# A depthwise convolution's low diagonal tiles and sampled products, moved from GpSimd and ScalarE to VectorE

## The reference

```python
def conv_module(x, prev, w1, b1, dw, dwb, lng, lnb, w2, b2):
    h = jnp.dot(x, w1) + b1
    a, gt = jnp.split(h, 2, axis=-1)
    u = a * jax.nn.sigmoid(gt)
    ext = jnp.concatenate([prev.astype(u.dtype), u], axis=1)
    c = lax.conv_general_dilated(ext, dw[:, None, :], window_strides=(1,), padding='VALID',
                                 dimension_numbers=('NWC', 'WIO', 'NWC'), feature_group_count=D_MODEL)
    c = layer_norm(c + dwb, lng, lnb)
    y = jnp.dot(jax.nn.silu(c), w2) + b2
    return y, ext[:, -CONV_CTX:]
```

## Time and profile before

| | |
|---|---|
| median of 3 runs | 1351.56 us (1350.29 to 1352.23) |
| span of the profiled execution, first to last instruction | 1350.1 us |
| TensorE, share of the span | 93% |
| VectorE | 78% |
| ScalarE | 59% |
| GpSimd | 4% |
| the depthwise stage on VectorE | about 334 to 428 us |
| the experts, all eight | about 500 to 1340 us |

### The profile page before, as it was taken

One profiled execution on the slowest core, in us unless ns is written; L12 is line 12 of the kernel. 1 busy time (PEld: TensorE's weight loads), 2 busy tenths in 40 slices (PEclk: granted clock), 3 DMA queues, 4 the chain that ended last, 5 costly groups with the idle time before them and its releaser, 6 DMA issues.

```text
span 1350.1 us, 22286 instructions
## 1 busy us (share of the span) xinstructions
PE 1262.2 (93%) x8696; PEld 1174.4 (87%) x8696; DVE 1046.8 (78%) x1016; ACT 802.5 (59%) x901; POOL 56.5 (4%) x34
## 2 busy tenths in 40 slices
PE   6999999989875989999999999999999999999993
PEld 4899999979874869999998998998998998998992
DVE  6734343469998668889889889888888888888886
ACT  3533333354653456766776766776776776776771
POOL 0000000001642000000000000000000000000000
PEclk9999999999887989999999999999999999999997
DMA  9854444253030407998998998998998998998931
GB/s 276 266 172 157 159 158 150 60 158 105 13 121 32 156 32 237 370 358 284 370 361 277 367 363 278 366 363 275 367 363 279 366 350 292 365 366 282 366 140 37
DMA packets 249538, 332.66 MB, mean 246 GB/s; under 512 B 6404, under 2 KB 222820, under 8 KB 249450
## 3 DMA queue, kind: packets, MB, share of 16 engines
q1 hardware_dynamic: 249283, 331.28, 73.2%
q10 hardware_dynamic: 199, 0.62, 0.2%
HBM read 330.44 MB, written 2.84 MB: 247 GB/s over the span
## 4 chain that ended last, share of the span: by engine, by line
PE 80%; DVE 14%; ACT 3%; issue 2%; DMA 1%; DVEq 0%; ACTq 0%
PE bank L1068 35%; PE bank L1088 18%; PE bank L889 15%; PE bank L918 6%; DVE cacc L1321 5%; PE bank L1032 2%; PE bank L1077 1%; PE bank L838 1%; DVE w_lo L1165 1%; PE bank L1053 1%; ACT w_hi L543 1%; DVE acc L1469 1%; DMA spool<-in_state_pool_dram 1%; PE bank L874 1%; DVE uc_lo L1349 1%
## 5 line engine op out<-in xcount | busy, mean ns | idle before, releaser
L1165 DVE TENSOR_TENSOR w_lo<-raw,w_hi 128x2048 fp32r<-128x2048 f32 x309 | 707.9, 2292 | 200.7 <-ACT w_hi L543 200.1
L543 ACT CAST w_hi<-raw 128x2048 fp32r<-128x2048 f32 x309 | 590.9, 1913 | 260.2 <-PE bank L889 107.6
L1068 PE MATMUL bank<-w_hi,xg_hi 128*128 128x256 f32 x1408 | 401.6, 285 | 5.3 <-DVE acc L1469 3.6
L1068 PE MATMUL bank<-w_hi,xg_lo 128*128 128x256 f32 x1408 | 394.0, 280 | 0.0
L1068 PE MATMUL bank<-w_lo,xg_hi 128*128 128x256 f32 x1408 | 393.9, 280 | 0.0
L1068 PEld LDWEIGHTS bank<-w_hi,xg_hi 128*128 128x128 f32 x1408 | 265.4, 189 | 13.2 <-issue 8.9
L1068 PEld LDWEIGHTS bank<-w_lo,xg_hi 128*128 128x128 f32 x1408 | 266.0, 189 | 3.2
L1068 PEld LDWEIGHTS bank<-w_hi,xg_lo 128*128 128x128 f32 x1408 | 265.2, 188 | 0.0
L889 PE MATMUL bank<-x_hi,w_hi 128*128 128x304 f32 (+1 forms) x544 | 166.2, 305 | 8.5 <-DVE x_lo L1252 5.3
L889 PE MATMUL bank<-x_hi,w_lo 128*128 128x304 f32 (+1 forms) x544 | 164.3, 302 | 0.0
L889 PE MATMUL bank<-x_lo,w_hi 128*128 128x304 f32 (+1 forms) x544 | 163.6, 301 | 0.0
(11 more groups left out here) (191 smaller groups left out, 1337.8 us busy)
## 6 DMA issues: line engine op xcount, KB each, us to landing
raw<-in_moe_w_gate_dram SPq DMA_DIRECT2D x88, 1024.0 KB, 5.6
raw<-in_moe_w_up_dram SPq DMA_DIRECT2D x88, 1024.0 KB, 5.9
raw<-in_moe_w_down_dram SPq DMA_DIRECT2D x88, 1024.0 KB, 5.2
raw<-in_conv_w_dram SPq DMA_DIRECT2D x12, 1024.0 KB, 5.4
raw<-in_ffn_w_gate_dram SPq DMA_DIRECT2D x11, 1024.0 KB, 8.0
raw<-in_ffn_w_up_dram SPq DMA_DIRECT2D x11, 1024.0 KB, 8.1
raw<-in_ffn_w_down_dram SPq DMA_DIRECT2D x11, 1024.0 KB, 4.9
poolw<-in_pool_w_dram SPq DMA_DIRECT2D x1, 1024.0 KB, 11.1
```

The lines of the kernel that those rows point to most:

```text
L543: act.copy(w_hi[t % SPLIT][:], raw[t % RAW][:]).then_inc(hi_ready, 1)
L1068: last = pe.matmul(bank[:, 0:TW], x[:, c, :], w[:, c, :], start=(c == 0 and k == 0), stop=(c == KC - 1 and k == 2))
L1165: dve.tensor_tensor(w_lo[t % SPLIT][:], raw[t % RAW][:], w_hi[t % SPLIT][:], ALU.subtract).then_inc(split_ready, 1)
```

## The change

GpSimd's part and ScalarE's low set are removed. VectorE now builds the low parts of all eight diagonal sets by the same whole-tile multiply and computes the sampled products of all eight chunks itself, in one buffer. The semaphores between GpSimd and VectorE (`prod_done`, `prod_used`) are gone; TensorE waits for one low tile more by count. The chunks of samples are taken in their own order. A low set waits for the same events as before. Sets 0 to 2 stand between the first instructions behind the product, sets 3 to 7 each at the head of one of the first five steps of the loop. Three taps of chunks 2 and 3, ahead of the loop before, move behind it, so 14 instructions stand after the bias and not 8.

```diff
-        prod = area("prod", [P, 2, NS, TAPS], F32, 2 * XB)
+        prod = area("prod", [P, 1, NS, TAPS], F32, 2 * XB)
...
-            pool.wait_ge(dw_lo_ready, 1)
-            plan = ["d0", "d1", "d2", "p0", "d3", "d4", "p1", "d6", "p2", "d7", "p3", "p4"]
-            for step in plan:
-                j = int(step[1])
-                if step[0] == "d":
-                    q, k0, k1 = DIAGS[j]
...
-                    pool.tensor_tensor(out, ident[:].unsqueeze(1).to_broadcast([P, k1 - k0, P]),
-                                       dw_lo[:, k0:k1, q - Q0:q - Q0 + 1].to_broadcast([P, k1 - k0, P]),
-                                       ALU.mult).then_inc(diag_lo_done, 1)
-                else:
...
-                    sampled_windows(pool, j, 0).then_inc(prod_done, 1)
...
-                if j in ACT_DIAGS:
-                    for k in range(k0, k1):
-                        last = act.mul(w_lo[diag_slot(j)][:, (k - k0) * P:(k - k0 + 1) * P], ident[:],
-                                       dw_lo[:, k, q - Q0:q - Q0 + 1])
                 last.then_inc(diag_hi_done, 1)
...
-                pe.wait_ge(diag_lo_done, j + 1 - sum(a <= j for a in ACT_DIAGS))
+                pe.wait_ge(diag_lo_done, j + 1)
...
+            def diag_low(j):
+                q, k0, k1 = DIAGS[j]
+                if j < SPLIT:
+                    dve.wait_ge(tile_used, T_W2 + j - SPLIT + 1)
+                else:
+                    dve.wait_ge(diag_used, j - SPLIT + 1)
+                out = w_lo[diag_slot(j)][:, 0:(k1 - k0) * P].rearrange("p (k m) -> p k m", m=P)
+                dve.tensor_tensor(out, ident[:].unsqueeze(1).to_broadcast([P, k1 - k0, P]),
+                                  dw_lo[:, k0:k1, q - Q0:q - Q0 + 1].to_broadcast([P, k1 - k0, P]),
+                                  ALU.mult).then_inc(diag_lo_done, 1)
+
             def sum_windows(c):
-                if c < POOL_CHUNKS:
-                    dve.wait_ge(prod_done, c + 1)
-                    dve.tensor_reduce(cacc[:, c, SEQ:NM], prod[:, 0], AX.X, ALU.add).then_inc(prod_used, 1)
-                else:
-                    link(sampled_windows(dve, c, 1))
-                    link(dve.tensor_reduce(cacc[:, c, SEQ:NM], prod[:, 1], AX.X, ALU.add))
+                link(sampled_windows(dve, c, 0))
+                link(dve.tensor_reduce(cacc[:, c, SEQ:NM], prod[:, 0], AX.X, ALU.add))
 
+            diag_low(0)
             uc_low(0)
+            diag_low(1)
             uc_low(1)
             convolve(0, TAPS - taps_done[0])
-            convolve(1, 3)
+            diag_low(2)
             uc_low(2)
             uc_low(3)
-            for c in (5, 0, 6, 1, 7, 2, 3, 4):
+            for c in range(KC):
+                if c < len(DIAGS) - SPLIT:
+                    diag_low(c + SPLIT)
                 convolve(1, 3)
                 sum_windows(c)
-            dve.wait_ge(prod_used, POOL_CHUNKS)
             dve.tensor_tensor(cacc[:, :, SEQ:NM], cacc[:, :, SEQ:NM],
```

More of the change, by code:

```diff
@@ L257, in build_trunk @@
         conv_out = sem("conv_out")
-        prod_done = sem("prod_done")
-        prod_used = sem("prod_used")
         routed = sem("routed")
@@ L343, in build_trunk @@
         DIAGS = [(q, k0, min(k0 + 16, TAPS)) for q in range(Q0, KC) for k0 in (0, 16)]
-        POOL_CHUNKS = 5
-        ACT_DIAGS = (5,)
         def diag_slot(j):
@@ L495, in _ @@
             pool.memset(uext[:, :, 0:CCTX], 0.0).then_inc(ctx_zeroed, 1)
-            pool.wait_ge(dw_lo_ready, 1)
-            plan = ["d0", "d1", "d2", "p0", "d3", "d4", "p1", "d6", "p2", "d7", "p3", "p4"]
-            for step in plan:
-                j = int(step[1])
-                if step[0] == "d":
-                    q, k0, k1 = DIAGS[j]
-                    if j < SPLIT:
-                        pool.wait_ge(tile_used, T_W2 + j - SPLIT + 1)
-                    else:
-                        pool.wait_ge(diag_used, j - SPLIT + 1)
-                    out = w_lo[diag_slot(j)][:, 0:(k1 - k0) * P].rearrange("p (k m) -> p k m", m=P)
-                    pool.tensor_tensor(out, ident[:].unsqueeze(1).to_broadcast([P, k1 - k0, P]),
-                                       dw_lo[:, k0:k1, q - Q0:q - Q0 + 1].to_broadcast([P, k1 - k0, P]),
-                                       ALU.mult).then_inc(diag_lo_done, 1)
-                else:
[L512 to L516, removed]
-                    sampled_windows(pool, j, 0).then_inc(prod_done, 1)
             pool.wait_ge(var_done, 4)
@@ L1350, in uc_low @@
                                   ALU.subtract).then_inc(uc_lo_done, 1)
-            def sum_windows(c):
-                if c < POOL_CHUNKS:
-                    dve.wait_ge(prod_done, c + 1)
-                    dve.tensor_reduce(cacc[:, c, SEQ:NM], prod[:, 0], AX.X, ALU.add).then_inc(prod_used, 1)
-                else:
-                    link(sampled_windows(dve, c, 1))
-                    link(dve.tensor_reduce(cacc[:, c, SEQ:NM], prod[:, 1], AX.X, ALU.add))
+            def diag_low(j):
[8 more added lines that the diff above has]
+                                  ALU.mult).then_inc(diag_lo_done, 1)
+            def sum_windows(c):
+                link(sampled_windows(dve, c, 0))
+                link(dve.tensor_reduce(cacc[:, c, SEQ:NM], prod[:, 0], AX.X, ALU.add))
+            diag_low(0)
             uc_low(0)
+            diag_low(1)
             uc_low(1)
             convolve(0, TAPS - taps_done[0])
-            convolve(1, 3)
+            diag_low(2)
             uc_low(2)
             uc_low(3)
-            for c in (5, 0, 6, 1, 7, 2, 3, 4):
+            for c in range(KC):
+                if c < len(DIAGS) - SPLIT:
+                    diag_low(c + SPLIT)
                 convolve(1, 3)
                 sum_windows(c)
-            dve.wait_ge(prod_used, POOL_CHUNKS)
             dve.tensor_tensor(cacc[:, :, SEQ:NM], cacc[:, :, SEQ:NM],
```

## The result

The changed kernel takes 1341.02 us (median of 4 runs, 1340.11 to 1342.29) against 1350.92 for the kernel before in the same session; the ratio is 0.9926, 95% interval 0.9914 to 0.9938. That is 9.9 us faster. The forecast was 1344.4, 7.2 us faster, in a range from 1341.8. The direction was right, and so was what it said of the stage that the change touches; the size of the whole was not. Of the 3.4 us between 1344.4 and 1341.02, 2.7 are gain that the sum did not have, and 0.6 come from the time of the kernel before, taken as 1351.56 in the forecast. The missing gain came from a place that the sum had left alone. The profiled executions differ by more, 1350.1 and 1339.1 us of span, and this 11.0 can be laid out piece by piece.

A forecast was written before the change was run, and what follows sets the result against it. VectorE's chain through the depthwise stage was taken as the bound: -38.8 + 17.2 + 10.9 + 0.6 + 2.3 = -7.8 us. Gain 7.9 at the subtraction, less 0.7 in the squares: 1351.56 - 7.2 = 1344.4 us, range 1341.8 to 1347.8.

The forecast's parts named there:

- VectorE is the chain, and GpSimd's multiplies hold it: Depthwise stage: VectorE carries the chain of waits; its instructions with two SBUF inputs stand still during GpSimd's multiplies.
- Removed stalls, 38.8 us: VectorE in the depthwise stage: 33.0 us of stalls in 120 taps and 5.8 in the `uc_lo` pair go.
- Added low sets, 2.21 and 2.08 each: VectorE builds eight low sets, four at each time, priced from the `w_lo` row: 17.2 us added.
- Rival B: Low sets on VectorE: repeated input costs 3.9 us a set, 14.0 us more on the chain; 1357.7 us, chance 0.06.
- Added products, 2.18 each: VectorE computes five more sampled products: 10.9 us added, plus 0.6 us for waits around the sums.
- The new pause, 2.3 us: After the 24 taps VectorE idles 2.3 us, waiting for the sigmoid before the last two chunks' `uext`.
- End of the convolution: VectorE is through with the convolution at 420.0 us, not 427.8: the terms sum to -7.8 us.
- TensorE is not late at the fourth low set: Low set 3: TensorE's set 0 ends at 357.2, VectorE arrives at 357.6, so 0.4 us of cover.
- Rival A: TensorE takes part back, by squares or set 0 at low clock, 2.8 to 4.3 us; 1347.2 us, chance 0.09.
- The mean: Norm's mean: only eight matmuls follow the convolution instead of 16, subtraction near 423.5, gain there 7.9 us.
- Rival D: Norm: the mean's eight matmuls run at high clock, no loss in the squares; gain 9.1, 1342.5 us, chance 0.07.
- What VectorE saves or adds there moves the norm, the second product and the experts behind it by as much.: Depthwise stage: VectorE's saving passes whole to everything behind it, since these are released one after the other.

The follow-up runs named there:

- a third with the short matmuls: The changed kernel plus 14 short matmuls of constants in TensorE's pauses around the gather of the first expert's rows: 1339.82 us, ratio 0.9909 to the kernel before.
- the products alone: The kernel before with all sampled products on VectorE; GpSimd keeps low sets 0 to 4, 6 and 7, ScalarE set 5: 1340.34 us, ratio 0.9914.
- the tiles alone: The kernel before with all eight low sets built by VectorE; GpSimd keeps the sampled products of chunks 0 to 4: 1348.90 us, ratio 0.9968.
- the kernel with ScalarE's four sets: The changed kernel with the low parts of sets 4 to 7 built on ScalarE, VectorE building only sets 0 to 3: 1331.97 us, ratio 0.9850.
- another arrangement of the program: The changed kernel with low parts of sets 4 to 7 on ScalarE and 14 short matmuls around the gather: 1330.44 us, ratio 0.9848.

## Why the prediction was off

- *VectorE is the chain, and GpSimd's multiplies hold it.* Right, shown from both sides: without them no tap lasts more than 485 ns; with six useless ones put back the stage grows by 19.9 us.
- *Removed stalls, 38.8 us.* Right. The mean of all taps fell from 750 ns to about 478, 32.6 us for 33.0, and the `uc_lo` pair fell to two of 0.45.
- *Added low sets, 2.21 and 2.08 each.* Right: 2.21 and 2.07 from start to start. The repeated input cost VectorE nothing here: 2.29 us to the end, as for the dense split. Rival B is out.
- *Added products, 2.18 each.* Nearly: from 2.19 down to 1.93. Together some 0.5 us less than counted, for the five added.
- *The new pause, 2.3 us.* Right, 2.34.
- *End of the convolution.* Forecast 85.9 us after the start of the 24 taps (420.0 - 334.09); measured 420.26 - 334.70 = 85.6.
- *TensorE is not late at the fourth low set.* Right, but not by the working. The transposes, counted at 3.24 us, ran faster and did not set the pace; TensorE waited for `uc_lo` behind them. Set 0 ended when ScalarE was released, at 356.65, 1.6 us ahead of VectorE and not 0.4. Rival A did not happen. The rows of TensorE and ScalarE in the changed kernel answer to the earlier trace rows:

```profile
347.93 1.92 PE L932 MATMUL bank<-ident,uext 128*30 128x128 f32 x16 [1.89 <-DVE uext L1311]
```

```profile
356.65 4.51 ACT L629 ACTIVATE w_hi<-ident,vec 128x128 fp32r<-128x128 f32 x15 [3.67 <-PE bank L943]
```

- *The mean.* Forecast gain 7.9, measured 7.56, since the second group took 4.17 us rather than 3.3. I had divided the 6.67 us of the group of 16 evenly. Its last matmuls had already run at the higher clock (granted 0.50 until 429.0 us, 0.82 from there to 431.4), and the first eight cost more than half. The 0.417 us that the forecast called the low pace was thus a mixture; eight in 4.17 us are 0.52 each. That is 0.8 us off, and it is half hidden by the products. Rival D's condition, these eight at the high clock, did not come true; that its 1342.5 lies nearest to the measured time is luck.
- *The squares, a loss of 0.7.* None: 4.15 us in both kernels, at a granted clock of 1.00, pause or not.
- *"What VectorE saves or adds there moves the norm, the second product and the experts behind it by as much."* This is the step that failed. It holds for the instructions but not for their durations. 4.1 us of the kernel before were lost to a clock of 1.2 GHz at the gather (4.59 for 3.02 us) and in the first block of the first expert (8.46 for 5.92), and the changed program is granted 2.4 GHz there. The term was not in the sum, neither as gain nor as loss, and rival D, which held the only larger gain, spoke of the mean instead. In the trace of before it could have been seen that something was to be gained or lost there: twelve matmuls of line 1032 at 4.6 us, in a stretch of clock 0.66, behind a pause. That this change would gain it could not be read from there.

What the runs leave open is why these shifts bring the high clock and others do not. The whole change, 7.6 us shorter in the stage, has it in two profiles of two, and in a third with the short matmuls; the products alone, 9.65 shorter, do not in their one profile; the tiles alone, 0.6 shorter, do not; the kernel with ScalarE's four sets does. So it is not the length of the shift alone. Leaving the kernels with short matmuls aside, the gather was slow where it started at 482.6, 494.1 (two kernels), 495.8 and 507.7 us and fast at 478.9, 485.8, 487.1 and 489.4. The place in time may still decide, by a rule that these nine profiles do not show. I cannot forecast the fall from these rows, only say what it cost here: about 4 us at this place.

## What to carry to other kernels

Two engines that both look idle enough can still stand in each other's way: before a multiply between SBUF tensors is given to GpSimd, or when one is there already, compare VectorE's mean duration with its median (750 against 475 ns here), and price the move as what VectorE loses while it runs, not as free help. Moving only the products, or moving the tiles on to ScalarE, whose instructions did not slow VectorE, was worth as much as or more than the whole change. And when a program is shifted in time, look through the rest of the chain for places where TensorE runs at the low clock behind a pause; a few spare matmuls there were worth 3.7 us of the kernel before, and the range of a forecast must hold such a gain or loss.

## What the runs showed of the hardware

- In this kernel a multiply of GpSimd with two SBUF inputs held a VectorE instruction with two SBUF inputs until its end: a tap of 0.475 us lasted up to 4.13, and the holding goes both ways, since GpSimd's 4.0 us product counted 5.7 when VectorE was ahead of it. Sums (`TENSOR_REDUCE`) took 1.17 to 1.19 us everywhere, also at 361.17 us of the kernel with only the products moved, where GpSimd's row of two multiplies runs from 358.53 to 368.19. The Trainium skill, "SBUF — State Buffer", section "Who interferes with whom", says that the port pair which the two engines share is an exclusive lock, that a VectorE instruction with two SBUF inputs contends with a GpSimd instruction that reads SBUF, and that a reduce never contends on trn2; the rows agree in all three.
- VectorE's multiply with both inputs in strides of 32 bytes took 1.93 to 2.19 us for 992 elements, with a dense and a repeated input 2.29 for 2048.
- ScalarE's taps of 128 elements took 0.30 us each in the low sets (4.48 for 15) and cost VectorE nothing: beside them no tap of VectorE lasted more than 0.486 us.
- The kernel before scattered over 8 us between its 34 executions in one session (1345.7 to 1353.9), another arrangement of the program over 1.2 in four (1330.0 to 1331.2). The mean granted clock was 0.971 to 0.977 in the former and 0.985 to 0.988 in the latter.
